# A hybrid encoder trunk on one core: first norm and turns re-ordered, tiles of x moved 384 columns apart

## The chip, the cores and the metric

The kernel runs on one core of a Trainium2 chip. The metric is the device time of one execution in microseconds, taken as the median of three runs. TensorE is called PE here, VectorE DVE, ScalarE ACT, GpSimd POOL and SyncE SP, as in the profile.

## The reference

Two layers, each a mixer and a squared-ReLU MLP, run over 1,024 prompt frames and 32 sample frames together, 1,056 columns in all. Cut to what matters:

```python
def trunk(x, ...):                      # DEPTH = 2, D_MODEL = 1024, D_FF = 4096
    for l in range(DEPTH):
        hn = rmsnorm(x, norm_mix_pre[l])
        m = mixer_even(hn, ...) if l % 2 == 0 else mixer_odd(hn, ...)
        x = x + rmsnorm(m, norm_mix_post[l])
        hn = rmsnorm(x, norm_ffn_pre[l])
        f = square(relu(hn @ mlp_up[l])) @ mlp_down[l]
        x = x + rmsnorm(f, norm_ffn_post[l])

def mixer_even(h, ...):                 # w_in: 1024 x 2048
    u, v, xb, gb = split(h @ w_in, 4)
    a_out = gelu(u) * spatial_gating(rmsnorm(gelu(v)))
    xc = causal_dwconv(xb, conv_w) + conv_b
    r, ig = sigmoid(xc @ wa + ba), sigmoid(xc @ wx + bx)      # block-diagonal
    log_a = -8 * r * softplus(-lam)
    h = scan(a=exp(log_a), b=sqrt(-expm1(2 * log_a)) * ig * xc)
    return concat(a_out, h * gelu(gb)) @ w_out

def mixer_odd(h, ...):                  # w_in: 1024 x 3072
    bg, cg, xv = split(h @ w_in, 3)
    return (bg * causal_dwconv(cg * xv)) @ w_out
```

## The kernel before

Activations lie transposed, features on the 128 partitions. The 1,056 columns are three tiles of 352 (`NT`, `TT`), the 1,024 features eight chunks (`KC`). Every float32 product is made of three passes in the faster `float32r` format: high weight by high x, high weight by low x, low weight by high x (L661 to L663). A **unit** is one output chunk of one tile: 8 x 3 = 24 matmuls of 128x352 into one of six PSUM banks. `plan()` lists 552 units and 184 weight panels. Most panels run over tiles 0, 1 and 2 in turn. Where a block starts or ends, four panels run together, first their tile 0, then tile 1, then tile 2 (a **tile block**). 104 of the 184 panels read the normed activations from `x_hi` and `x_lo` (16 of the even mixer, 32 of each MLP, 24 of the odd mixer). The rest read `h_hi` and `h_lo`. In each of the four buffers a chunk's row is `TS` = 1,088 columns, and tile t starts 352 t columns (1,408 t bytes) into it.

Each engine walks the units in order. The order of all else is written out by hand as tables of (unit, step), where step i follows the i-th of a unit's eight chunks: `COL_AT` (a norm's column sums on PE), `GATE_STEPS` (gate matmuls), `CONV_AT`, `DECAY_AT`, `SCAN_AT` (on DVE, with ACT's part), and the functions `even_unit`, `turn_before` and `turn_after`. An engine that waits in its program holds back all that stands behind it. For unit n DVE first evacuates the bank (`evacuate`), then makes the low part of a weight panel if one is due (`low`), then does what `even_unit` or `turn_after` names. PE needs the bank of unit n-6 evacuated and its panel's low part (`w_ready`).

A norm of x goes: ACT squares (`x_squares`), DVE sums eight chunks to one and folds them (`x_sum`, `rs_fold`), PE sums over the partitions (`col_sums`), ACT takes the root (`rs_root`), DVE the reciprocal and a transpose that spreads it (`rs_inverse`). x's own high and low parts are made beside this (`x_part` on ACT, `x_low` on DVE), since the norm's factor is applied when the bank is evacuated.

In the even mixer's beginning DVE convolves (`convolve`, 4 operations of 1,059 columns), PE makes six gate matmuls per group through one bank, each waiting until ACT has taken the sigmoid of the one before, ACT makes exp and tanh (`decays`), DVE the drive (`decay`), ACT a root (`drive_root`), DVE the scan. ACT's `gelu_panel(0)` works on units 12 to 14 and waits for their evacuation. `softplus` is 22 tiny dependent DVE operations. `BLOCK[b]` is the first unit of the last tile block before a turn to the next norm; s counts units from it, and s = 12 is the next phase's first unit.

Of the kernel before, what the change touches and what calls it, by code (L numbers as in the profile page):

```python
# [159 lines left out]
def build(nc, A, O):  # L161
# [27 lines left out]
    with ExitStack() as ctx:  # L189
# [51 lines left out]

        x_hi_raw = place("x_hi_raw", [P, KC * TS], F32, at_x_hi)
        x_old = place("x_old", [P, KC * TS], F32, at_x_lo)
# [5 lines left out]
        spare = [x_hi_raw[:, k * TS + TOK:k * TS + TOK + NJ] for k in range(KC)]  # L249
        fold, root, rcol = spare[0:6], spare[6], spare[7]  # L250
# [29 lines left out]
        v_out_s = place("v_out_s", [DEC, HALF], F32, at_h_lo + 8192)  # L280
# [151 lines left out]
        for b in range(4):  # L432
            for i, (what, t) in enumerate([("post", 0), ("post", 1), ("pre", 0), ("post", 2), ("pre", 1), ("pre", 2)]
# [17 lines left out]
        GATE_STEPS = (((10, 5), (11, 0), (11, 3), (11, 6), (12, 1), (12, 4)),  # L451
# [4 lines left out]
        DECAY_AT = (12, 17, 23, 31)  # L456
        SCAN_AT = (14, 18, 24, 32)
# [30 lines left out]

        block = ctx.enter_context(nc.Block())

        @block.sync
        def _(sp):
            def source(l):
                name, i = LOADS[l].name
                if name == "w_in_even":
                    return A[name][LOADS[l].col]
                w = A[name][i]
                return w[LOADS[l].row:LOADS[l].row + D, LOADS[l].col * P:LOADS[l].col * P + P]

# [19 lines left out]
            def first_half(l):  # L519
                sp.dma_start(W[l][2][:, 0:4, :], source(l)[:, 0:4, :]).then_inc(w_first[l], 16)  # L520
# [63 lines left out]
        def _(pool):  # L584
# [22 lines left out]
            for n in TMP_NO:  # L607
# [18 lines left out]
                else:  # L626
# [7 lines left out]
                                            ALU.subtract).then_inc(y_ready, 1)  # L634


        @block.tensor
        def _(pe):
# [133 lines left out]
            def warm_up(a):  # L772
                nc.tensor.matmul(ps[:, a, 0:TT], tmp[0][:, 0:P], tmp[0][:, :], start=True, stop=True)
# [62 lines left out]
        def _(act):  # L836
# [11 lines left out]
            def x_squares(u, t):  # L848
                for h in range(2):
                    if u > 0:  # L850
                        act.wait_ge(x_new, 6 * (u - 1) + 2 * t + h + 1)
                        dst = part(x_old, 4 * h, 4 * h + 4, t)
# [49 lines left out]
            def turn_before(n):  # L902

                for b in range(4):
# [16 lines left out]
                    if s == 13:  # L921
                        rs_root(b, "pre", 1)
                        x_squares(b + 1, 2)
                    if s == 15:
                        rs_root(b, "pre", 2)

            def turn_after(n):
                for b in range(3):
# [5 lines left out]
                    if s == 13:  # L934
                        x_part(b + 1, 2, 0, 8)
# [15 lines left out]
            x_squares(0, 1)  # L951
            act.wait_ge(consts, 3)
# [713 lines left out]
```

## Time and profile before

| | |
|---|---|
| median of 3 runs | 2172.08 us (2171.65 to 2172.17) |
| the profiled execution, its own time | 2171.2 us |
| its span | 2168.7 us |
| PE busy | 2153.3 us, 99% |
| DVE busy / ACT busy / POOL busy | 910.4 / 653.6 / 89.2 us |
| mean granted clock of PE | 0.998 |

The span runs from the first to the last instruction; 2.5 us of the execution lie around it. PE's busy share is an upper bound on its usefulness, since its matmuls overlap (each lasts some 320 ns and starts some 159 ns after the one before). The time that an extra wait costs is read from the starts.

### The profile page before, as it was taken

The numbers are of one execution on the slowest core, as the hardware profiler recorded it, in microseconds if no ns is written. First come the engines' busy times: TensorE is split into PE (matmuls) and PEld (weight loads), VectorE is DVE, ScalarE is ACT, GpSimd is POOL, SyncE is SP. The second block draws the span as 40 slices with busy tenths as digits, with TensorE's granted clock in tenths as the row PEclk, the third lists the DMA queues.
The fourth block names the chain that finished last, engine by engine and source line by source line (L and its number), as shares of the span: only waits on it lengthen the run. The fifth ranks groups of instructions, "written<-read, shape, count | busy, mean of one in ns | idle before, by whom it ended". The sixth has DMA issues, their size and how long they took to land.

```text
span 2168.7 us, 31484 instructions
## 1 busy us (share of the span) xinstructions
PE 2153.3 (99%) x13496; PEld 2140.8 (99%) x13496; DVE 910.4 (42%) x1438; ACT 653.6 (30%) x1105; POOL 89.2 (4%) x102
## 2 busy tenths in 40 slices
PE   8999999999999999999999999999999999999998
PEld 8999999999999999999999999999999999999998
DVE  7766367323322322333953333393223223322336
ACT  5673345202311320233511112353013103202332
POOL 0000000000000000000032332000000000000000
PEclk9999999999999999999999999999999999999999
DMA  4111422111111111132311113221111111111142
GB/s 159 34 37 40 139 76 83 50 49 44 45 49 49 44 45 49 49 104 74 114 49 46 49 49 130 66 92 53 46 50 49 41 48 49 49 40 49 49 139 81
DMA packets 208409, 138.64 MB, mean 64 GB/s; under 512 B 6000, under 2 KB 204784, under 8 KB 208272
## 3 DMA queue, kind: packets, MB, share of 16 engines
q1 hardware_dynamic: 207840, 136.04, 20.6%
q8 instruction: 107, 1.75, 0.3%
q10 hardware_dynamic: 432, 0.60, 0.1%
q14 instruction: 30, 0.25, 0.0%
HBM read 119.22 MB, written 17.40 MB: 63 GB/s over the span
## 4 chain that ended last, share of the span: by engine, by line
PE 96%; DVE 2%; issue 1%; ACT 1%; DMA 0%; DVEq 0%; SPq 0%; ACTq 0%
PE ps L661 31%; PE ps L662 31%; PE ps L663 31%; PE ps L736 1%; DVE x_lo L1228 1%; DVE x_old L1217 0%; PE ps L764 0%; DMA w_all_raw<-in_w_in_even_dram 0%; PE ps L692 0%; DVE f L1206 0%; PE ps L679 0%; PE ps L683 0%; PE ps L747 0%; DVE f L1199 0%; ACT L1032 0%
## 5 line engine op out<-in xcount | busy, mean ns | idle before, releaser
L661 PE MATMUL ps<-x_hi,w_all 128*128 128x352 f32 x2304 | 748.9, 325 | 0.0
L662 PE MATMUL ps<-x_lo,w_all 128*128 128x352 f32 x2304 | 740.7, 321 | 0.0
L663 PE MATMUL ps<-x_hi,w_all 128*128 128x352 f32 x2304 | 740.6, 321 | 0.0
L661 PE MATMUL ps<-h_hi,w_all 128*128 128x352 f32 x1728 | 556.2, 322 | 0.0
L663 PE MATMUL ps<-h_hi,w_all 128*128 128x352 f32 x1728 | 555.2, 321 | 0.0
L662 PE MATMUL ps<-h_lo,w_all 128*128 128x352 f32 x1728 | 555.2, 321 | 0.0
L661 PEld LDWEIGHTS ps<-x_hi,w_all 128*128 128x128 f32 x2304 | 432.9, 188 | 2.8 <-issue 0.3
L662 PEld LDWEIGHTS ps<-x_lo,w_all 128*128 128x128 f32 x2304 | 433.1, 188 | 2.4 <-issue 0.3
L663 PEld LDWEIGHTS ps<-x_hi,w_all 128*128 128x128 f32 x2304 | 432.9, 188 | 0.0
L839 ACT CAST w_all<-w_all_raw 128x1024 fp32r<-128x1024 f32 x166 | 173.4, 1044 | 531.9 <-DMA w_all_raw<-in_mlp_down_dram 324.2
L661 PEld LDWEIGHTS ps<-h_hi,w_all 128*128 128x128 f32 x1728 | 324.5, 188 | 0.3 <-DVE h_lo L1433 0.3
L662 PEld LDWEIGHTS ps<-h_lo,w_all 128*128 128x128 f32 x1728 | 324.5, 188 | 0.0
L663 PEld LDWEIGHTS ps<-h_hi,w_all 128*128 128x128 f32 x1728 | 324.4, 188 | 0.0
L1268 DVE SCALAR_TENSOR_TENSOR tmp<-ps,rstd 128x352 f32<-128x352 f32 x192 | 100.5, 524 | 424.6 <-PE ps L663 424.6
L898 ACT ACTIVATE tmp<-tmp 128x352 f32<-128x352 f32 x192 | 95.7, 498 | 473.0 <-DVE tmp L1268 472.5
L1274 DVE TENSOR_TENSOR f<-ps,f 128x352 f32<-128x352 f32 x144 | 75.4, 523 | 359.8 <-PE ps L663 359.8
L1167 DVE TENSOR_TENSOR w_all<-w_all_raw,w_all 128x1024 fp32r<-128x1024 f32 x166 | 202.1, 1217 | 14.7 <-ACT w_all L839 14.7
L1248 DVE TENSOR_TENSOR h_lo<-tmp,h_hi 128x352 fp32r<-128x352 f32 x192 | 99.0, 516 | 1.2 <-ACT h_hi L900 1.2
L900 ACT CAST h_hi<-tmp 128x352 fp32r<-128x352 f32 x192 | 93.6, 487 | 6.1
L1271 DVE COPY f<-ps 128x352 f32<-128x352 f32 x48 | 25.2, 525 | 138.0 <-PE ps L663 138.0
L1243 DVE TENSOR_TENSOR sq_sum<-sq_sum,tmp 128x352 f32<-128x352 f32 x83 | 43.3, 521 | 81.7 <-ACT tmp L891 79.7
L663 PE MATMUL ps<-h_hi,x_hi 128*128 128x352 f32 x192 | 61.7, 321 | 0.0
(192 smaller groups left out, 1430.9 us busy)
## 6 DMA issues: line engine op xcount, KB each, us to landing
w_all_raw<-in_mlp_up_dram SPq DMA_DIRECT2D x60, 512.0 KB, 3.9
w_all_raw<-in_mlp_down_dram SPq DMA_DIRECT2D x60, 512.0 KB, 3.7
x_save<-f SPq DMA_DIRECT2D x9, 1408.0 KB, 5.9
x_old<-x_save SPq DMA_DIRECT2D x9, 1408.0 KB, 11.6
w_all_raw<-in_c_w_in_dram SPq DMA_DIRECT2D x22, 512.0 KB, 3.6
w_all_raw<-in_w_in_even_dram SPq DMA_DIRECT2D x12, 512.0 KB, 3.5
x_old<-in_x_cols_dram SPq DMA_DIRECT2D x3, 1408.0 KB, 12.4
w_all_raw<-in_w_out_even_dram SPq DMA_DIRECT2D x6, 512.0 KB, 3.7
```

The source lines that it names most:

```text
L661: nc.tensor.matmul(dst, wh, hi, start=(i == 0), stop=False)
L662: nc.tensor.matmul(dst, wh, lo, start=False, stop=False)
L663: last = nc.tensor.matmul(dst, wl, hi, start=False, stop=(i == KC - 1))
L839: nc.scalar.copy(W[l][0], W[l][2]).then_inc(w_high, 1)
L898: nc.scalar.activation(tmp[n % 3][:, :], tmp[n % 3][:, :], ACT.Square).then_inc(h_sq, 1)
L900: nc.scalar.copy(pt(h_hi, u.m, u.t), tmp[n % 3][:, :]).then_inc(h_high, 1)
L1167: nc.vector.tensor_tensor(lo, raw, hi.bitcast(F32), ALU.subtract).then_inc(w_ready, 1)
L1243: nc.vector.tensor_tensor(dst, dst, tmp[n % 3][:, :], ALU.add).then_inc(f_acc, 1)
L1248: nc.vector.tensor_tensor(pt(h_lo, u.m, u.t), tmp[n % 3][:, :], pt(h_hi, u.m, u.t).bitcast(F32), ALU.subtract).then_inc(h_ready, 1)
L1268: ins = nc.vector.scalar_tensor_tensor(tmp[n % 3][:, :], bank(n), 0.0, scale, ALU.max, ALU.mult)
L1271: ins = nc.vector.tensor_copy(pt(f, m, t), bank(n))
L1274: ins = nc.vector.tensor_tensor(pt(f, m, t), bank(n), pt(f, m, t), ALU.add)
```

## The change

1. **First norm.** ACT makes x's high part of tile 2 before the first root. DVE evacuates the first four units, then does in one stretch the sum of tile 1, the low part of tile 2 and the sum of tile 2. `softplus` moves from unit 7 to unit 9. The first and third column sums move a step earlier and two steps later.
2. **Even mixer's beginning.** The first gates move from units 10 to 12 to units 11 to 13, the first `decays`/`decay` from 12 to 13, the first scan from 14 to 15. `gelu_panel(0)` stays at 14.
3. **Turns** (three of them). The squares of tile 2 go to the free h buffer and no longer onto `x_lo`'s place, so the low part need not wait for their sum; it goes first. ACT's root for tile 2 moves from s = 15 to 18, DVE's reciprocal from 15 to 20, PE's column sum from (20, 4) to (21, 5).
4. **Start.** The first two half panels are loaded by DMAs that ACT issues, around `vecs`; SP issues the rest.
5. **End.** Four small copies move from DVE to POOL.
6. **Layout.** In `x_hi` and `x_lo` a tile starts 384 columns (1,536 bytes) after the one before, a row is `XS` = 1,152 columns, and the sums of squares (`sq_sum`), `fold`, `root` and `rcol` live in the 32-column gaps. `h_hi`, `h_lo` and `f` keep their layout.

```diff
+XS = TOK + 96
-        x_hi = place("x_hi", [P, KC * TS], F32R)
+        x_hi = place("x_hi", [P, KC * XS], F32R)
-        x_lo = place("x_lo", [P, KC * TS], F32R)
+        x_lo = place("x_lo", [P, KC * XS], F32R)
-        spare = [x_hi_raw[:, k * TS + TOK:k * TS + TOK + NJ] for k in range(KC)]
-        fold, root, rcol = spare[0:6], spare[6], spare[7]
+        gap_hi, gap_lo = [b[:, :].rearrange("p (g n) -> p g n", g=NT * KC)[:, :, TT:TT + QUAD] for b in (x_hi_raw, x_old)]
+        sq_sum = (gap_hi[:, 0:NJ], gap_hi[:, NJ:2 * NJ], gap_lo[:, 0:NJ])
...
+        def tile_at(buf, t):
+            return t * (TT + QUAD if buf.shape[1] == KC * XS else TT)
...
-                     ("pre", 1): (16, 2), ("pre", 2): (20, 4)}
+                     ("pre", 1): (16, 2), ("pre", 2): (21, 5)}
-        COL_AT.update({(5, 1): (-1, "pre", 0), (7, 1): (-1, "pre", 1), (8, 5): (-1, "pre", 2)})
+        COL_AT.update({(5, 0): (-1, "pre", 0), (7, 1): (-1, "pre", 1), (8, 7): (-1, "pre", 2)})
-        GATE_STEPS = (((10, 5), (11, 0), (11, 3), (11, 6), (12, 1), (12, 4)),
+        GATE_STEPS = (((11, 4), (11, 7), (12, 2), (12, 5), (13, 0), (13, 3)),
-        DECAY_AT = (12, 17, 23, 31)
-        SCAN_AT = (14, 18, 24, 32)
+        DECAY_AT = (13, 17, 23, 31)
+        SCAN_AT = (15, 18, 24, 32)
...
             first_x(0, 0, 2, 0)
-            first_half(0)
             first_x(1, 2, 4, 0)
-            for l in range(1, 4):
-                first_half(l)
+            for l in range(2, 4):
+                first_half(sp, l)
...
+            first_half(act, 0)
             act.dma_start(vecs[:, :], A["vecs"]).then_inc(v_in, 16)
+            first_half(act, 1)
...
+                        if t == 2:
+                            act.wait_ge(pe_unit, START[u])
+                        dst = part((x_old, x_old, h_hi_raw)[t], 4 * h, 4 * h + 4, t)
...
             x_part(0, 1, 0, 8)
             x_squares(0, 1)
+            x_part(0, 2, 0, 8)
             act.wait_ge(consts, 3)
             rs_root(-1, "pre", 0)
-            x_part(0, 2, 0, 8)
             x_squares(0, 2)
...
-                if n == 0:
+                if n == 3:
                     x_sum(0, 1)
-                if n == 1:
                     x_low(0, 2, 0, 8)
-                if n == 2:
+                    x_sum(0, 2)
                     rs_inverse(-1, "pre", 1)
-                if n == 3:
-                    x_sum(0, 2)
                 if n == 7:
+                    rs_inverse(-1, "pre", 2)
+                if n == 9:
                     softplus()
-                    rs_inverse(-1, "pre", 2)
...
-                    if s == 15:
+                    if s == 20:
                         rs_inverse(b, "pre", 2)
...
                     if s == 14:
-                        x_sum(b + 1, 2)
                         x_low(b + 1, 2, 0, 8)
                         if UNITS[n - 1].kind == "up":
                             h_low(n - 1)
+                    if s == 15:
+                        x_sum(b + 1, 2)
```

**DVE, the first units, before.** Evacuations of the first twelve units write `xb_pad`; `sq00` and `sq01` are the squares of tiles 2 and 1 (tile 0's too, earlier), `x_lo` the low parts, the RECIPROCAL the third norm's, `soft` the first row of `softplus`, `lru0` the first convolution, `w_all` the low part of panel 4, which unit 12 needs.

```order
L1280 TENSOR_TENSOR xb_pad_79<-ps,rstd_57 128x352
L1217 TENSOR_TENSOR sq01_75<-sq01_75 128x1408
...
L1228 SCALAR_TENSOR_TENSOR x_lo_50<-f_53,vecs_64,x_hi_49 128x352 x8
...
L1217 TENSOR_TENSOR sq00_74<-sq00_74 128x1408
...
L1186 TENSOR_REDUCE x_hi_raw_70<-sq_sum_56 128x11
L1280 TENSOR_TENSOR xb_pad_79<-ps,rstd_57 128x352 x4
L1148 TENSOR_SCALAR soft_65<-soft_65 128x4
...
L1173 RECIPROCAL x_hi_raw_70<-x_hi_raw_70 128x11
L1175 STREAM_TRANSPOSE rstd_57<-x_hi_raw_70 128x352
L1280 TENSOR_TENSOR xb_pad_79<-ps,rstd_57 128x320
...
L1349 TENSOR_SCALAR lru0_86<-xb_pad_79,vecs_64 128x1059
...
L1167 TENSOR_TENSOR w_all_54<-w_all_raw_55,w_all_54 128x1024
```

**The same engine and place, in the change.** Line numbers are those of the changed kernel.

```order
L1291 TENSOR_TENSOR xb_pad_78<-ps,rstd_59 128x352 x4
L1230 TENSOR_TENSOR sq01_74<-sq01_74 128x1408
...
L1241 SCALAR_TENSOR_TENSOR x_lo_50<-f_53,vecs_63,x_hi_49 128x352 x8
L1230 TENSOR_TENSOR sq00_73<-sq00_73 128x1408
...
L1200 TENSOR_REDUCE x_old_70<-x_old_70 128x11
L1187 RECIPROCAL x_old_70<-x_old_70 128x11
...
L1291 TENSOR_TENSOR xb_pad_78<-ps,rstd_59 128x352 x4
L1187 RECIPROCAL x_old_70<-x_old_70 128x11
...
L1360 TENSOR_SCALAR lru0_85<-xb_pad_78,vecs_63 128x1059
...
L1162 TENSOR_SCALAR soft_64<-soft_64 128x4
...
L1181 TENSOR_TENSOR w_all_54<-w_all_raw_55,w_all_54 128x1024
```

Four evacuations stand together ahead of both sums, and `softplus` and with it everything behind stands between the first convolution and panel 4's low part.

**ACT, units 12 to 16, before.** `lru3`, `lru1` are exp and tanh (L988, L990) and then the root (L995) of the first group; `tail` the copies of conv rows; `gelu0` is `gelu_panel(0)`; the CAST is a weight panel's high part; `ig1` the first gate of the second group (L979).

```order
L988 ACT_TABLE_LOAD
L988 ACTIVATE lru3_89<-lru1_87,soft_65 128x1059
L990 ACTIVATE lru1_87<-lru1_87,soft_65 128x1059
L839 CAST w_all_54<-w_all_raw_55 128x1024
L995 ACT_TABLE_LOAD
L995 ACTIVATE lru1_87<-lru1_87 128x1059
L967 COPY tail_66<-xb_pad_79 128x3
...
L1032 ACT_TABLE_LOAD
L1032 ACTIVATE gelu0_93<-gelu0_93 128x1056
L839 CAST w_all_54<-w_all_raw_55 128x1024
L979 ACT_TABLE_LOAD
L979 ACTIVATE ig1_92<-ps,vecs_64 128x353 x2
```

**The same in the change.** The root of the first group (L1009) now stands behind the gelu (L1046), which waits for unit 14's evacuation; DVE has the first `decay` ahead of that evacuation, where before it had it ahead of unit 13's.

```order
L1002 ACT_TABLE_LOAD
L1002 ACTIVATE lru3_88<-lru1_86,soft_64 128x1059
L1004 ACTIVATE lru1_86<-lru1_86,soft_64 128x1059
L981 COPY tail_65<-xb_pad_78 128x3
...
L1046 ACT_TABLE_LOAD
L1046 ACTIVATE gelu0_92<-gelu0_92 128x1056
L1009 ACT_TABLE_LOAD
L1009 ACTIVATE lru1_86<-lru1_86 128x1059
L849 CAST w_all_54<-w_all_raw_55 128x1024
L993 ACT_TABLE_LOAD
L993 ACTIVATE ig1_91<-ps,vecs_63 128x353 x2
```

**DVE, a turn, before:** from the evacuation of unit s = 14 (`tmp2`) on. `x_old` holds the squares of tile 2, `x_lo` gets tile 2's low parts, the RECIPROCAL is `rs_inverse(b, "pre", 2)`, and the row behind it is unit s = 15's evacuation.

```order
L1268 SCALAR_TENSOR_TENSOR tmp2_60<-ps,rstd_57 128x352
L1217 TENSOR_TENSOR x_old_71<-x_old_71 128x4x352
...
L1219 TENSOR_TENSOR sq_sum_56<-x_old_71 128x352
L1186 TENSOR_REDUCE x_hi_raw_70<-sq_sum_56 128x11
L1228 SCALAR_TENSOR_TENSOR x_lo_50<-f_53,vecs_64,x_hi_49 128x352 x8
L1248 TENSOR_TENSOR h_lo_52<-tmp1_59,h_hi_51 128x352
L1173 RECIPROCAL x_hi_raw_70<-x_hi_raw_70 128x11
...
L1268 SCALAR_TENSOR_TENSOR tmp0_58<-ps,rstd_57 128x352
```

**The same in the change.** The low parts stand ahead of the sum, the squares are in `h_hi_raw`, and the RECIPROCAL has moved behind the evacuation of unit s = 19.

```order
L1279 SCALAR_TENSOR_TENSOR tmp2_58<-ps,rstd_59 128x352
L1241 SCALAR_TENSOR_TENSOR x_lo_50<-f_53,vecs_63,x_hi_49 128x352 x8
L1259 TENSOR_TENSOR h_lo_52<-tmp1_57,h_hi_51 128x352
L1279 SCALAR_TENSOR_TENSOR tmp0_56<-ps,rstd_59 128x352
...
L1230 TENSOR_TENSOR h_hi_raw_71<-h_hi_raw_71 128x4x352
...
L1233 TENSOR_TENSOR x_old_70<-h_hi_raw_71 128x11x32
L1200 TENSOR_REDUCE x_old_70<-x_old_70 128x11
L1279 SCALAR_TENSOR_TENSOR tmp1_57<-ps,rstd_59 128x352
...
L1187 RECIPROCAL x_old_70<-x_old_70 128x11
```

## Rows read from the trace of the kernel before

**Rows 1.** The page, busy time, share of the span and instructions of PE.

```profile
PE 2153.3 (99%) x13496; PEld 2140.8 (99%) x13496; DVE 910.4 (42%) x1438; ACT 653.6 (30%) x1105; POOL 89.2 (4%) x102
```

**Rows 2.** Timeline, PE, 39 to 62 us: start, us, what, idle before and releaser.

```profile
42.99 0.36 PE L723 MATMUL ps<-x_hi_raw,quads 128*128 128x11 f32 x2 [1.16 <-issue]
...
55.61 1.51 PE L736 MATMUL ps<-lru,gate_w 128*128 128x353 f32 x2 [4.54 <-issue]
```

**Rows 3.** Windows: length, busy of PE, PEld, DVE, ACT, POOL, granted clock, DMA.

```profile
53.40:60.20 6.80, 4.59 (x13) 3.87 (x14) 3.85 (x7) 1.49 (x2) 0.00 (x0) 0.50 0.09 7
```

**Rows 4.** Windows over two units of tile 0, then three of tile 1.

```profile
328.81:336.41 7.60, 7.60 (x51) 7.60 (x49) 7.31 (x13) 5.73 (x11) 0.00 (x0) 1.00 0.77 235
340.45:351.97 11.52, 11.52 (x74) 11.52 (x73) 10.83 (x14) 7.88 (x13) 0.00 (x0) 1.00 0.34 127
```

**Rows 5.** Timeline, ACT, around the first root.

```profile
28.05 0.27 ACT L845 ACTIVATE x_hi_raw<-ps,eps 128x11 f32<-128x11 f32 x1 [4.11 <-PE ps L723]
28.22 3.94 ACT L866 ACTIVATE x_hi<-f,vecs 128x352 fp32r<-128x352 f32 x8
```

**Rows 6.** Timeline, DVE, 28 to 60 us.

```profile
28.61 0.55 DVE L1175 STREAM_TRANSPOSE rstd<-x_hi_raw 128x352 f32<-128x352 f32 x1
...
33.70 4.04 DVE L1228 SCALAR_TENSOR_TENSOR x_lo<-f,vecs,x_hi 128x352 fp32r<-128x352 f32 x8
...
39.22 2.53 DVE L1217 TENSOR_TENSOR sq<-sq 128x1408 f32<-128x1408 f32 x2
...
42.82 1.78 DVE L1280 TENSOR_TENSOR xb_pad<-ps,rstd 128x352 f32<-128x352 f32 x4
...
48.98 0.23 DVE L1173 RECIPROCAL x_hi_raw<-x_hi_raw 128x11 f32<-128x11 f32 x1
...
50.60 0.83 DVE L1349 TENSOR_SCALAR lru<-xb_pad,vecs 128x1059 f32<-128x1059 f32 x1
...
55.42 0.58 DVE L1280 TENSOR_TENSOR xb_pad<-ps,rstd 128x320 f32<-128x320 f32 x2
...
59.42 1.22 DVE L1167 TENSOR_TENSOR w_all<-w_all_raw,w_all 128x1024 fp32r<-128x1024 f32 x1
```

**Rows 7.** Timeline, PE, two gate matmuls of unit 16.

```profile
82.50 0.75 PE L736 MATMUL ps<-xc,gate_w 128*128 128x353 f32 x2
...
84.53 0.76 PE L736 MATMUL ps<-xc,gate_w 128*128 128x353 f32 x2
```

**Rows 8.** Timeline, DVE, the first drive.

```profile
70.71 1.25 DVE L1358 TENSOR_TENSOR lru<-lru,lru 128x1059 f32<-128x1059 f32 x1
...
73.22 1.26 DVE L1363 SCALAR_TENSOR_TENSOR lru<-lru,lru 128x1059 f32<-128x1059 f32 x1 [0.58 <-ACT lru L990]
...
77.61 0.52 DVE L1292 TENSOR_TENSOR gelu<-ps,rstd 128x352 f32<-128x352 f32 x1
```

**Rows 9.** Timeline, ACT, gelu, a panel's cast, a table load, the first gate of unit 16.

```profile
79.73 1.09 ACT L1032 ACTIVATE gelu<-gelu 128x1056 f32<-128x1056 f32 x1 [0.74 <-DVE gelu L1292]
81.41 1.05 ACT L839 CAST w_all<-w_all_raw 128x1024 fp32r<-128x1024 f32 x1 [0.59 <-DMA w_all_raw<-in_w_in_even_dram]
82.48 1.28 ACT L979 ACT_TABLE_LOAD   x1
83.78 0.56 ACT L979 ACTIVATE ig<-ps,vecs 128x353 f32<-128x353 f32 x1
```

**Rows 10.** Timeline, PE, first turn, from unit s = 20 to s = 21.

```profile
355.88 0.32 PE L663 MATMUL ps<-x_hi,h_lo 128*128 128x352 f32 x1
356.36 0.40 PE L661 MATMUL ps<-x_hi,h_hi 128*128 128x352 f32 x1 [0.16 <-DVE tmp L1268]
```

**Rows 11.** Timeline, DVE, the four small copies of the end.

```profile
2162.08 0.73 DVE L1599 COPY row_rstd<-x_hi_raw 32x2 f32<-32x2 f32 x4
```

**Rows 12.** Timeline, POOL, two products of the same shape in the odd mixer.

```profile
1156.49 0.96 POOL L630 TENSOR_TENSOR cy<-tmp,cy 128x352 f32<-128x352 f32 x1 [6.68 <-DVE cy L1483]
...
1159.02 1.97 POOL L630 TENSOR_TENSOR cy<-tmp,cy 128x352 f32<-128x352 f32 x1
```

More of the change, by code:

```diff
@@ L240, in build @@
         last_rstd = row_rstd[:, 0:2]
-        x_hi_raw = place("x_hi_raw", [P, KC * TS], F32, at_x_hi)
-        x_old = place("x_old", [P, KC * TS], F32, at_x_lo)
+        x_hi_raw = place("x_hi_raw", [P, KC * XS], F32, at_x_hi)
+        x_old = place("x_old", [P, KC * XS], F32, at_x_lo)
         h_hi_raw = place("h_hi_raw", [P, KC * TS], F32, at_h_hi)
         h_lo_raw = place("h_lo_raw", [P, KC * TS], F32, at_h_lo)
-        spare = [x_hi_raw[:, k * TS + TOK:k * TS + TOK + NJ] for k in range(KC)]
-        fold, root, rcol = spare[0:6], spare[6], spare[7]
+        gap_hi, gap_lo = [b[:, :].rearrange("p (g n) -> p g n", g=NT * KC)[:, :, TT:TT + QUAD] for b in (x_hi_raw, x_old)]
+        sq_sum = (gap_hi[:, 0:NJ], gap_hi[:, NJ:2 * NJ], gap_lo[:, 0:NJ])
+        fold = [gap_lo[:, NJ + i, 0:NJ] for i in range(6)]
+        root, rcol = gap_lo[:, NJ + 6, 0:NJ], gap_lo[:, NJ + 7, 0:NJ]
         sq0 = [place(f"sq0{i}", [P, KC, TT], F32, at_h_lo + i * KC * TT * 4) for i in range(2)]
@@ L279, in build @@
                 cy.append(place(f"cy{n}{i}", [P, TOK], F32, at + 2 * TOK * 4 + 2 * c_step + i * TOK * 4))
-        v_out_s = place("v_out_s", [DEC, HALF], F32, at_h_lo + 8192)
+        v_out_s = place("v_out_s", [DEC, HALF], F32, at_h_lo + 13056 + HALF * 4)
         def chunk_buf(bufs, c):
@@ L487, in send_rows, with source, first_half @@
                 eng.dma_start(O["y_rows"][i, :, h * HALF:(h + 1) * HALF], result_rows(i, h)).then_inc(out_dma, 16)
+        def source(l):
+            name, i = LOADS[l].name
+            if name == "w_in_even":
+                return A[name][LOADS[l].col]
+            w = A[name][i]
+            return w[LOADS[l].row:LOADS[l].row + D, LOADS[l].col * P:LOADS[l].col * P + P]
+        def first_half(eng, l):
+            eng.dma_start(W[l][2][:, 0:4, :], source(l)[:, 0:4, :]).then_inc(w_first[l], 16)
         block = ctx.enter_context(nc.Block())
@@ L634, in _ @@
                                             ALU.subtract).then_inc(y_ready, 1)
+            pool.wait_ge(inverted, NORM[3, "post", 2] + 1)
+            for b in range(4):
+                nc.gpsimd.tensor_copy(last_rstd[b * QUAD:(b + 1) * QUAD, :],
+                                      rcol[b * QUAD:(b + 1) * QUAD, 3 + b::4]).then_inc(last_r, 1)
         @block.tensor
@@ L772, in warm_up @@
             def warm_up(a):
-                nc.tensor.matmul(ps[:, a, 0:TT], tmp[0][:, 0:P], tmp[0][:, :], start=True, stop=True)
+                nc.tensor.matmul(ps[:, a, 0:TT], rstd[:, 0:P], rstd[:, 0:TT], start=True, stop=True)
             def out_rows(i, a):
@@ L1212, in squares @@
                 def squares(k0, k1):
-                    return part(x_old, k0, k1, t) if u > 0 else sq0[t % 2][:, k0:k1, :]
+                    return part((x_old, x_old, h_hi_raw)[t], k0, k1, t) if u > 0 else sq0[t % 2][:, k0:k1, :]
                 for i, h in enumerate((4, 2)):
@@ L1218, in x_sum @@
                     dve.wait_ge(x_tree, n + i + 1)
-                nc.vector.tensor_tensor(sq_sum[:, t * TT:(t + 1) * TT].unsqueeze(1), squares(0, 1), squares(1, 2), ALU.add
-                                        ).then_inc(x_acc, 1)
+                a, c = [squares(k, k + 1).rearrange("p o (j c) -> p (o j) c", c=QUAD) for k in range(2)]
+                nc.vector.tensor_tensor(sq_sum[t], a, c, ALU.add).then_inc(x_acc, 1)
                 rs_fold(u - 1, "pre", t)
             def x_low(u, t, k0, k1):
-                if u > 0:
+                if u > 0 and t < 2:
                     dve.wait_ge(x_acc, 3 * u + t + 1)
@@ L1319, in second_low @@
                                         ).then_inc(w_ready, 1)
-            nc.vector.memset(tmp[0][:, :], 0.0).then_inc(warm, 1)
+            nc.vector.memset(rstd[:, 0:TT], 0.0).then_inc(warm, 1)
             dve.wait_ge(w_first[0], 16)
@@ L1597, in _ @@
             nc.vector.tensor_tensor(c, c, part(x_old, 0, KC, 2, 0, LAST_COLS), ALU.add).then_inc(x_new, 1)
-            for b in range(4):
-                nc.vector.tensor_copy(last_rstd[b * QUAD:(b + 1) * QUAD, :],
-                                      rcol[b * QUAD:(b + 1) * QUAD, 3 + b::4]).then_inc(last_r, 1)
             dve.wait_ge(last_r, 4)
```

53 lines of the change are left out of this document (19 added, 34 removed).

## The prediction

> **What bounds the kernel now.** I read the busy times first: PE is busy 99% of the span [rows 1], and no other engine comes to half of it. So every part of the change has to be told by the starts of PE's matmuls. Where these stand at their steady distance nothing done on DVE, ACT or POOL counts. The second view was the windows by tile. Two units of tile 0 take 7.60 us, 3.80 a unit or 158.4 ns a matmul. Three units of tile 1 take 11.52 us, 3.84 a unit or 160.0 ns [rows 4]. The busy share is full in both, so this is a pace and no wait, and the difference, 0.040 us a unit, goes with the tile whose row starts 1,408 bytes into the chunk. The third view was the timeline of the first 90 us, where PE does wait: 1.16 us ahead of the column sum at (8, 5) and 4.54 us ahead of the gate at (10, 5) [rows 2]. Around and behind the second the granted clock is 0.50 for 6.80 us in which PE worked 4.59 us [rows 3], so half of that work, 2.3 us, is lost as well. Last come the turns, where one start is late by 0.48 - 0.16 = 0.32 us behind an evacuation [rows 10], and the end, where four small copies take 0.73 us on DVE [rows 11].
>
> **Beginning, first half.** I followed DVE's new order with the durations of before. The first root started at 28.05, behind a column sum [rows 5]. ACT now makes the eight high parts of tile 2 (3.94 us) ahead of it, in the 4.11 us that it stood idle, so they cost nothing and the squares of tile 2 are ready earlier. With the column sum one step earlier the reciprocal and transpose (28.61 to 29.16 before) end at about 28.9. Then on DVE: four evacuations 1.8 to 30.7; a sum with its fold 3.6 (2.53 for its two large additions, the rest for the last addition and the fold) to 34.3; eight low parts 4.0 to 38.3; the second sum 3.6 to 41.9 [rows 6]. The column sum now stands at (8, 7). PE would have reached (8, 5) at 42.99 - 1.16 = 41.8; two chunks of 0.48 later, and 0.2 earlier for the start, is 42.6. So the 1.16 us wait goes, and PE enters unit 9 at 42.8. DVE goes on: reciprocal, transpose and four evacuations 2.6 to 44.5; then reciprocal, transpose and the evacuation of unit 8, another 1.6 with PE's column sum waited for at 42.6, to 46.1; the first convolution 4.8 (50.60 to 55.42) to 50.9. The gate at (11, 4) is reached at 42.8 + 7.6 + 2.4 = 52.8, behind that: the 4.54 us wait goes too [rows 2, 6].
>
> **A wait takes its place.** Unit 12 needs the low part of panel 4, and `softplus` now stands ahead of it. Between 44.6 and 48.98 DVE did `softplus` and nothing else, 4.4 us [rows 6]. So: evacuation of unit 9 to 51.4, `softplus` to 55.9, evacuation of 10 to 56.4, low part 1.22 to 57.6. A gate adds (84.53 - 82.50) - 9 x 0.16 = 0.6 us to PE [rows 7]. PE comes to unit 12 at 42.8 + 7.6 + 3.8 + 1.2 = 55.4 and waits until 57.75, **2.4 us**.
>
> **A second wait.** Units 12 and 13 take 10.0 with two gates each: PE is through unit 13 at 67.75. DVE: its evacuation to 68.4, the low part of panel 6 to 69.5, the first `decay` 6.3 us (70.71 to about 77.0, its 0.58 us wait for ACT included) to 75.85, the evacuation of unit 14 to 76.35 [rows 8]. Before, this `decay` stood ahead of unit 13's evacuation, with the same gelu behind unit 14's. ACT: the gelu 1.09 to 77.45; a table load of 1.28 and the root, of 1,059 columns too, 1.09 to 79.85; the cast 1.05 to 80.9; another table load 1.28 to 82.2; the second group's first gate 0.56 to 82.75 [rows 9]. PE's next gate, (16, 4), needs that one's bank: it starts at 82.85. PE is there at 67.75 + 7.6 + 3.0 = 78.35, and waits **4.5 us**. Queued behind ACT's gelu are the root, the cast and every gate's sigmoid, and behind PE's gate the whole of unit 16. The same gate stood at 84.53 before [rows 7]. So of the 6.2 us (84.53 - 78.35) that the first half gives, **1.7 are left**.
>
> **The clock.** Before, PE lost 2.3 us to the half clock, and all of it lies ahead of the gate of unit 16, so it is in the 84.53 already. The new 4.5 us wait can bring a fall of its own behind it: nothing (the 1.16 us wait brought none) to 2.3 us (as much as the 4.54 us wait did, of like length) [rows 2, 3]. The fall of before began some 2.3 us into the idle time and reached 4.6 us past it, so I take **+1.5**. The 2.4 us wait ahead of unit 12 lies between 1.16 and 4.54. A fall there is absorbed by the second wait, up to 4.5 us, so it costs 0.
>
> **Pace.** In the change tile 1 starts 1,536 bytes into a chunk's row. 104 panels read `x_hi` and `x_lo`, and each has one unit of tile 1. Five of them (four in the first block, and unit 13) lie ahead of the second wait, which swallows what they gain. If the tile's place in memory sets the pace, 99 x 0.040 = **-4.0 us** [rows 4]. The bounds are 0 (the pace belongs to the tile's number or its output) and -4.0. I take the whole, since everything else about the two kinds of unit is the same: the weights, the number of columns, the engine loads. The products of `h_hi` and `h_lo` keep their places and their pace.
> The Trainium skill has a rule that speaks against this term: "TensorE: Matmul & The Clock Gate", section "Back-to-back issue gap", puts the distance of two warm matmuls at their columns over 2.4 plus 2.5 ns, with nothing about where the moving rows lie. That would be an estimated 149 ns for both tiles and no gain; the rows show 158.4 and 160.0, so the rule does not describe the difference that is there.
>
> **Turns.** The row shows a start 0.32 us late, since the evacuation of s = 15 stands behind the RECIPROCAL, and that behind ACT's root [rows 10]. In the change the low parts do not wait for the sum, and the RECIPROCAL has gone to s = 20. Three turns like this give 1.0, and the shorter stretch of DVE before it some more at the start of the same block (0 to 0.2 each): **-1.2** (bounds 0, if the sum at s = 15 makes another evacuation late, and -1.6). The column sum now stands at (21, 5), five units or 19 us after the evacuation of s = 15; the sum and its fold, 3.6 us, and ACT's root lie between the two, and that distance hides them.
>
> **End.** The four copies, 0.73 us [rows 11], leave DVE. POOL has nothing else to do there, and may make them while DVE still multiplies, or 0.73 us in parallel and then be waited for. **-0.7** at best; the low bound is 0. POOL's product took 1.97 us beside DVE's two-input operation and 0.96 alone [rows 12], so POOL may be the later one.
> The Trainium skill, "SBUF — State Buffer", section "SBUF: two separate sides", says that GpSimd and a two-input operation of DVE lock each other out of the shared port. The trace agrees (0.96 against 1.97). By that rule the copies would overlap DVE's last large additions badly and the term would be some -0.2 by estimate.
>
> **Start.** Two half panels of 256 KB go out from ACT rather than from SP. The bytes are the same and PE's first matmul waits for the last of them: 0 to -0.5, I take -0.2, which runs through the whole chain above.
>
> **Sum.** Against the execution's own 2171.2 us, of which the median of 2172.1 is 0.9 more: -1.7 - 0.2 + 1.5 - 4.0 - 1.2 - 0.7 = -6.3, so 2164.9 of its own and **2165.8 us** as a median. A measurement of this kernel tells about 0.2%, 4.3 us: the edges are 2167.7 and 2176.4.
>
> **Rivals.**
> - The second wait does not come (`decay` or the gelu is through earlier than I count, or the chain behind the gelu is shorter). Then the beginning gives 6.2 us and no clock is lost: 2172.1 - 6.4 - 4.0 - 1.2 - 0.7 = 2159.8. For it: my chain has eleven links. Against it: each has its row. 0.13.
> - The layout changes no pace: 2165.8 + 4.0 = 2169.8. For it: the rows show only that pace goes with tile. 0.12.
> - The clock falls as deep and long at both waits as before, and the second fall is not covered: 2.3 rather than 1.5 behind it, and 1.7 more where the first fall outlasts the slack: 2168.3. 0.09.
> - Slower: 1,408 is not what costs, but any start other than one that follows the last row without a gap, or the longer row itself. All tiles of x then take 3.84 us: 208 units of tiles 0 and 2 x 0.040 = +8.3 in place of -4.0, so 2178.1. It decides from a pace of tiles 0 and 2 above 3.83 us, where the loss outweighs the other terms and the edge of 0.2% (4.3 us, and 2.3 for the gain of the other terms, are 6.6 over 208 units, 0.032 each). Against it: tile 2 starts 2,816 bytes in and has tile 0's pace. 0.04.
>
> **How the numbers follow.** The forecast has 0.62; its own range is 2163.5 to 2168.0 (start and end terms at zero; clock 0 to 2.3). The whole range, 2159.8 to 2169.9, takes in the case without a second wait and the case of no change in pace. Faster: 0.62 less a little, 0.13, and a third of the clock's case, 0.78; within 0.2%: 0.17; slower 0.05.
>
> **What would show it.** PE's starts at units 12 and (16, 4): idle 2.4 and 4.5 us, the first behind DVE's low part, the second behind ACT's gate, with no idle time at (8, 7) and (11, 4). The window over three units of tile 1 of an x panel: 11.40 us rather than 11.52. The start after s = 20: 0.16. PE's clock behind the second wait. In the end DVE's last additions followed by less than 0.73 us. I am wrong if the first `softplus` row is not followed by a wait of unit 12, if ACT's gelu of unit 14 isn't late, or if tile 1 keeps 3.84.

## The result, and the profile after

The changed kernel takes 2191.78 us (median of 4 runs, 2191.51 to 2192.01), against 2171.86 us beside it. The ratio is 1.0093, with a 95% interval of 1.008 to 1.0106: **slower by 0.9%**, some 20 us, where 2165.8 was forecast with a range up to 2169.9.

The page, busy time, share of the span and instructions, as in [rows 1]:

```profile
PE 2176.1 (99%) x13496; PEld 2164.0 (99%) x13496; DVE 911.5 (42%) x1434; ACT 652.5 (30%) x1105; POOL 90.8 (4%) x106
```

PE has the same number of instructions and is busy all the time, 22.8 us longer. So the loss is no wait. Windows over whole units of the changed kernel, with the columns of [rows 3]:

```profile
371.57:403.57 32.00, 32.00 (x194) 32.00 (x193) 11.06 (x19) 11.68 (x20) 0.00 (x0) 1.00 0.17 50
1164.97:1196.97 32.00, 32.00 (x193) 32.00 (x193) 8.19 (x15) 4.79 (x9) 10.46 (x10) 1.00 0.17 50
...
511.32:522.72 11.40, 11.40 (x75) 11.40 (x73) 3.14 (x5) 2.92 (x5) 0.00 (x0) 1.00 0.17 47
```

The first two windows are eight units each of x, in the first MLP and in the odd mixer. They take 4.00 us a unit, tiles 0, 1 and 2 alike, at a granted clock of 1.00. The third is one panel of x in the first MLP's second group, with the same instructions on the same buffers: 3.80 us a unit, and tile 1's among them, where [rows 4] had 3.84. Away from the column sums the starts of the slow units stand 165 to 168 ns apart, 166.7 on average. Timeline, PE, changed kernel, in the odd mixer:

```profile
1164.97 0.33 PE L671 MATMUL ps<-x_hi,w_all 128*128 128x352 f32 x1
1165.14 0.33 PE L672 MATMUL ps<-x_lo,w_all 128*128 128x352 f32 x1
1165.31 0.33 PE L673 MATMUL ps<-x_hi,w_all 128*128 128x352 f32 x1
1165.47 0.33 PE L671 MATMUL ps<-x_hi,w_all 128*128 128x352 f32 x1
```

So PE has three rhythms here: 158.4 ns (its distances go 155, 159, 158, 162), an even 160.0, and an even 166.7. The third was in the trace of before too, for part of one unit of tile 2 (the ninth), and I had not looked at it. Timeline, PE, kernel before:

```profile
39.51 0.33 PE L663 MATMUL ps<-x_hi,w_all 128*128 128x352 f32 x1
39.68 0.33 PE L661 MATMUL ps<-x_hi,w_all 128*128 128x352 f32 x1
39.84 0.33 PE L662 MATMUL ps<-x_lo,w_all 128*128 128x352 f32 x1
40.01 0.33 PE L663 MATMUL ps<-x_hi,w_all 128*128 128x352 f32 x1
```

In the change the slow stretches are units 71 to 96 (into the first MLP), 263 to 336 (the whole odd mixer) and 359 to 384. Each begins behind the column sum at s = 10 of a turn and ends at the first unit of h's tile 1. Between the two spans, 2168.7 and 2190.1 us, the difference is made up like this (from the start of each unit's first matmul in the two traces):

| part | us |
|---|---|
| start: first steady unit later | +0.44 |
| from there to the end of the even mixer's input (unit 47) | +1.45 |
| 120 units of x at 4.00, with the turns that lie in them | +20.6 |
| 6 units of h at 4.00 | +1.2 |
| 48 free units of x's tile 1, 3.80 for 3.84 | -1.9 |
| behind the last unit | -0.3 |
| sum | +21.4 |

The two waits of the beginning came where they were forecast, the first at half its size. Timelines of the changed kernel, PE at unit 12 and at the gate (16, 4), ACT's gelu, root, cast and first gate behind it:

```profile
58.06 0.43 PE L671 MATMUL ps<-x_hi,w_all 128*128 128x352 f32 x1 [1.15 <-DVE w_all L1181]
...
83.13 1.54 PE L746 MATMUL ps<-xc,gate_w 128*128 128x353 f32 x2 [4.22 <-ACT ig L993]
```

```profile
76.79 1.08 ACT L1046 ACTIVATE gelu<-gelu 128x1056 f32<-128x1056 f32 x1 [4.01 <-DVE gelu L1303]
77.89 1.28 ACT L1009 ACT_TABLE_LOAD   x1
79.19 1.08 ACT L1009 ACTIVATE lru<-lru 128x1059 f32<-128x1059 f32 x1
80.18 1.03 ACT L849 CAST w_all<-w_all_raw 128x1024 fp32r<-128x1024 f32 x1
81.22 1.28 ACT L993 ACT_TABLE_LOAD   x1
82.52 0.56 ACT L993 ACTIVATE ig<-ps,vecs 128x353 f32<-128x353 f32 x1
```

The gate stands at 83.13 (forecast 82.85), 1.4 us ahead of [rows 7]. Behind it the clock falls; windows, changed kernel:

```profile
78.50:88.62 10.12, 5.90 (x21) 4.79 (x19) 8.10 (x7) 5.68 (x7) 0.00 (x0) 0.69 0.00 0
```

From that gate to the start of unit 17 PE took 5.5 us at a granted clock of 0.50, where before it took 2.8 at 1.00. That is 2.7 us for the clock, of which I had put down 1.5. So unit 17 starts 1.28 us later than before, instead of earlier.

### The profile page after: what moved, and what is told of

The parts are those of the page before. It is cut to its first block, busy times and chain, and to the rows that moved or that the text cites. A ratio compares the mean times of both kernels' runs of the same rounds, so it can differ in the third digit from the quotient of the medians.

```text
span 2190.1 us, 31486 instructions
## 1 busy us (share of the span) xinstructions
PE 2176.1 (99%) x13496; PEld 2164.0 (99%) x13496; DVE 911.5 (42%) x1434; ACT 652.5 (30%) x1105; POOL 90.8 (4%) x106
## 4 chain that ended last, share of the span: by engine, by line
PE 97%; DVE 2%; ACT 1%; issue 0%; DVEq 0%; ACTq 0%
PE ps L671 32%; PE ps L672 31%; PE ps L673 31%; PE ps L746 1%; PE ps L774 0%; PE ps L783 0%; PE ps L689 0%; PE ps L693 0%; PE ps L702 0%; DVE sq L1230 0%; DVE xb_pad L1291 0%; PE ps L757 0%; DVE x_lo L1241 0%; DVE lru L1364 0%; PE ps L733 0%
## 5 line engine op out<-in xcount | busy, mean ns | idle before, releaser
L672 PE MATMUL ps<-h_lo,x_hi 128*128 128x352 f32 x192 | 61.9, 322 | 0.0
```

The lines of the kernel that those rows point to most:

```text
L672: nc.tensor.matmul(dst, wh, lo, start=False, stop=False)
```

## The experiments

All addresses below are counted from the kernel's first buffer, and what is said of them is their remainder by 256 bytes. In before, x's and h's tiles stand at 0, 128, 0, and all weights at 128, but for the first block's fourth panel, at 0. In the change x's three tiles stand at 0; h and the weights are as before. `quads`, the weights of a column sum, stands at 32 before and at 128 in the change.

**Order alone, layout alone.** Two kernels: `order_only` is the change without its layout, `layout_only` before with nothing but that layout.

> The change's whole order (beginning, turns, start, end) on the layout of before: tiles of x 352 columns apart, sums of squares in a buffer of their own. Theory A (the layout does the harm: with every tile of x a whole number of 256 bytes from its chunk's start, PE's rhythm falls after a column sum into one of 166.7 ns a matmul and no tile-1 unit frees it): no unit of the first MLP or the odd mixer at 4.00 us, tile 1 at 3.84 again, about +1.3 us from the beginning, -1.1 from the turns, 2172.5 us in all. Theory B (the re-ordered turns let it in): the same 120 units at 4.00 us, about 2193 us.

> The new layout alone (tiles 384 columns apart, rows of 1,152, sums in the gaps), with before's order everywhere. Theory A: units 71 to 96, 263 to 336 and 359 to 384 at 4.00 us as in the change, +21.8 for them, -2.0 for the free tile-1 units, about 2192 us. Theory B: no unit at 4.00 us, every tile 3.80, about 2168 us.

`order_only`: 2171.1 us, ratio 0.9996 (0.9986 to 1.0005), every x unit at 3.80 or 3.84. So the re-ordering as a whole is worth nothing beyond the noise. In its trace two parts cancel: unit 17 starts 0.4 us later than before, and from unit 48 on the turns give 1.6 us. Unit 12 is waited for 1.82 us there. `layout_only`: median 2186.24, ratio 1.0053 (1.0032 to 1.0074), with executions from 2174 to 2195 us (one of 6411 us, and one of before of 4341 us, are left out of the ratios). The loss is the layout's, though not a fixed one: this kernel spreads over 21 us where the others of these comparisons agree within 5.

**The layout alone, a second profile.**

> The new layout alone on before's order once more, for a profile of an execution of ordinary length (its nine times ran from 2174 to 2195 us with one far outside). Theory A (with all tiles of x alike, a rhythm entered at a restart is never left before the next h tile 1): each stretch of x's units from a turn to the end of its phase stands as a whole at 4.00 or at 3.80 us a unit, and which it is differs from execution to execution; the time follows from the stretches: 2169 + 14 for the odd mixer + 4.6 for each MLP.

This execution took 2172.08 us. Its slow stretches are short: units 71 to 80, 263 to 272, 359 to 368. Timeline, PE, `layout_only_2`, inside unit s = 20 and the first matmuls of s = 21:

```profile
356.99 0.33 PE L664 MATMUL ps<-x_hi,h_hi 128*128 128x352 f32 x1
357.16 0.33 PE L665 MATMUL ps<-x_lo,h_hi 128*128 128x352 f32 x1
357.33 0.32 PE L666 MATMUL ps<-x_hi,h_lo 128*128 128x352 f32 x1
357.78 0.40 PE L664 MATMUL ps<-x_hi,h_hi 128*128 128x352 f32 x1
358.02 0.32 PE L665 MATMUL ps<-x_lo,h_hi 128*128 128x352 f32 x1
358.18 0.32 PE L666 MATMUL ps<-x_hi,h_lo 128*128 128x352 f32 x1
```

PE goes at 0.167 until 357.33, then starts 0.45 later, and from there at 158 ns. This is the late evacuation of [rows 10], the wait that the re-ordered turns take away. My expectation was that a stretch is slow or fast as a whole; it is not. A small pause can end it, and does so in all three turns of this execution. Not every interruption does: in the change the column sums at s = 13, 16 and 21 stand inside the slow stretch (the matmuls around them start 304 and 248 ns apart instead of 167), and 166.7 goes on behind each.

**Layout with the new turns.** Everything else is before's.

> The new layout and the re-ordered turns, with before's beginning, start and end. Theory A2 (the layout lets the slow rhythm stand; PE's wait of some 0.3 us at s = 21, which the new turns take away, was what ended it in the executions of the layout alone): units 71 to 96, 263 to 336 and 359 to 384 at 4.00 us in every execution, 2172 + 21.8 - 2.0 - 1.1 = 2191 us, with a spread of under 1 us. Rival (the turns have no part in it): as the layout alone, executions anywhere from 2172 to 2195 us.

2191.64 us (2190.93 to 2191.85), ratio 1.0094 (1.0077 to 1.0111): units 71 to 96, 263 to 336 and 359 to 384 slow, in executions within 1 us of each other. Windows, `layout_turns`, three units of the odd mixer:

```profile
1164.84:1176.84 12.00, 12.00 (x74) 12.00 (x73) 3.39 (x5) 3.46 (x6) 6.09 (x6) 1.00 0.16 45
```

So the turns, good for 0.3 us or more each by themselves, take away the pause that had at times ended the slow rhythm. The two parts of the change together cost more than the layout alone.

**Does the place set the pace?** Two kernels move x's buffers by 128 bytes (everything behind them by 256), in the change and in before.

```diff
+        at_byte[0] += 128
         at_x_hi = at_byte[0]
 ...
+        at_byte[0] += 128
         at_h_hi = at_byte[0]
```

> The changed kernel with x_hi and x_lo moved 128 bytes up and everything behind them 256 bytes, so that all three tiles of x start at an odd multiple of 128 bytes, as tile 1 alone did before, and h's tiles keep theirs. If the place within 256 bytes sets the pace of x's units: 3.84 us (160.0 ns a matmul) for all three tiles, none at 4.00, so -16 for the 120 slow units and +5.8 for the 144 that ran at 3.80: about 2181 us. If row length, gap or order set it: 4.00 us in the same 120 units and about 2192 us.

> The kernel before with x_hi and x_lo moved 128 bytes up and everything behind them 256 bytes; nothing else. If the place within 256 bytes sets the pace: x's units of tiles 0 and 2 take 3.84 us and those of tile 1 3.80, h's stay as they are: 208 x 0.04 - 104 x 0.04 = +4.2, about 2176 us. If the tile's number or its output sets it: no change, 2172 us.

`after_off`: 2181.41 us, x's units all at 3.84 in the MLPs and the odd mixer. `before_off`: 2178.09 us, ratio 1.0032 (1.0019 to 1.0045). Windows, `before_off`, the same panel of the odd mixer over its tiles 0, 1 and 2:

```profile
1196.93:1200.77 3.84, 3.84 (x26) 3.84 (x25) 1.30 (x2) 0.49 (x1) 3.18 (x3) 1.00 0.48 137
1200.77:1204.57 3.80, 3.80 (x26) 3.80 (x25) 0.53 (x1) 1.53 (x3) 1.29 (x2) 1.00 0.00 0
1204.57:1208.41 3.84, 3.84 (x26) 3.84 (x25) 1.66 (x2) 0.00 (x0) 0.00 (x0) 1.00 0.01 4
```

The tiles have changed roles: [rows 4] had 3.80 for tile 0 and 3.84 for tile 1. The place does set the pace. The 2 us above expectation are mostly 16 units of h at 4.00 (60 to 62, 67 and their like in the four turns). Some panels of h have their weights in x's buffer, and these had moved with it: unit 67 reads such a panel, and units 60 to 62 stand behind one.

**Against what?** The change, with the rotating weights and what lies behind them moved instead of the rows:

```diff
-        at_byte[0] += 128
         at_w = at_byte[0]
```

> The changed kernel without the 128 bytes between f and w_all, so that the weights of the rotating slots start at whole multiples of 256 bytes as x's tiles do, and nothing of the activations moves. If it is the place of moving rows against that of the weights that sets the pace: x's units on rotating slots 3.84 us and none at 4.00, h's tiles 0 and 2 on them 3.84 and h's tile 1 3.80, so -18 for the slow units, +8 for the free x units, +3 for h: about 2184 us. If only the moving rows' own place counts: as the changed kernel, 2192 us with 120 units at 4.00.

2183.32 us, ratio 1.0051 (1.0035 to 1.0068). Windows, `weights_off`, three x units of one panel, and h's tiles 0 and 1:

```profile
1200.57:1212.09 11.52, 11.52 (x74) 11.52 (x74) 3.45 (x5) 2.02 (x4) 4.45 (x4) 1.00 0.16 46
1548.08:1551.92 3.84, 3.84 (x26) 3.84 (x25) 0.52 (x1) 0.00 (x0) 0.00 (x0) 1.00 0.49 137
1551.92:1555.72 3.80, 3.80 (x27) 3.80 (x25) 0.53 (x1) 1.05 (x1) 0.00 (x0) 1.00 0.02 4
```

No row of x or h moved, and yet x is at 160 on all rotating slots and h's tiles have changed roles. So it is the place of the moving rows *against that of the weights*. Where both stand at the same place within 256 bytes, PE goes at 160.0. Where they stand 128 apart, it goes at 158.4 or at 166.7, and stays in either. This holds for all thirteen profiles of ordinary length. From unit 48 on, all 2,271 units with both at the same place are at 160.0. Of the 4,281 units with 128 between them 3,755 are at 158.4, 514 at 166.7, and 12 come out near 160, nine of them with a column sum in them. Other distances than 0 and 128 were not tried.

**What ends and what begins the slow rhythm?** In the change the third rotating slot alone goes 128 bytes up, so that x's panels on it are of the 160 kind:

```diff
-        w_all = place("w_all", [P, 6, D], F32R)
+        w_all = place("w_all", [P, 4, D], F32R)
+        at_byte[0] += 128
+        w_p2 = place("w_p2", [P, 2, D], F32R)
```

> The changed kernel with the third rotating slot alone moved 128 bytes up, so that every third panel of x has weights that stand to x's rows as they did to tile 1's before. If such a unit frees the slow rhythm: the x panels on that slot take 3.84 us, those on the other two 3.80, and no stretch of 4.00 is longer than two panels: about 2173 us. If the slow rhythm is a matter of the layout as a whole: units on the other two slots stay at 4.00 in the same stretches and the time is above 2185 us.

2202.91 us, ratio 1.014 (1.0125 to 1.0155): the slowest of all. Windows, `p2_off`, an MLP's panel on the second slot (after units of h), then one on the moved slot, then two on the others:

```profile
880.04:891.45 11.41, 11.41 (x75) 11.41 (x74) 3.14 (x5) 2.92 (x5) 0.00 (x0) 1.00 0.16 46
891.45:902.97 11.52, 11.52 (x74) 11.52 (x74) 4.01 (x7) 3.91 (x7) 0.00 (x0) 1.00 0.16 47
902.97:926.95 23.98, 23.98 (x145) 23.98 (x145) 8.02 (x14) 7.82 (x14) 0.00 (x0) 1.00 0.16 44
```

3.80, then 3.84, then six units at 4.00. A unit of the 160 kind does end a slow stretch, and no stretch is longer than two panels; that much was right. But such a unit also starts the next one, when the weights' place changes behind it while the rows' place stays. In before the 160 kind comes with tile 1, where the rows' place changes, and its next unit falls to 158.4. The thirteen profiles bear both out. Where a unit of the 160 kind is followed by one of the other kind because the *rows'* place changed, that one is at 158.4 in 1,281 of 1,285 cases. Where the *weights'* place changed, it is at 166.7 in 83 of 95 cases (`p2_off`, `weights_off`, `before_off`, `after_off`). The short slow stretches of the change's beginning (units 4 to 6 and 8 to 10) stand behind such a change of weights too, the panel at place 0. My time for this kernel was 30 us off, since I had no term for a new entry.

**What lets it in at s = 10?** The last matmuls of unit s = 10 behind the column sum stand 299, 247, 161 ns apart in the slow kernels and 303, 246, 162 in before. The same column sum; but `quads` stands elsewhere. (The column sum at s = 8, in units of the same kind, leaves 158.4 in all of them, with `quads` at 128 too. So the place alone is not enough, and what sets s = 10 apart from s = 8 was not tried.) So the change with `quads` where it was, within 256 bytes:

```diff
+        at_byte[0] += 160
         ident = place("ident", [P, P], F32)
         quads = place("quads", [P, P], F32)
```

> The changed kernel with ident, quads and what lies behind them 160 bytes up, so that the column sums' weights stand at the same place within 256 bytes as before. In the kernel before the same column sum at s = 10 goes back to 158 ns, in the change to 166.7. If the place of quads decides which rhythm follows a column sum: no unit at 4.00 us, 2192 - 21.8 = 2170 us. If not: units at 4.00 as in the change, 2192 us.

2167.34 us (2165.27 to 2168.97), ratio 0.998 (0.9971 to 0.999): **24.4 us less than the change**, by 160 bytes that nothing uses. It is also 3.8 us less than `order_only`, which differs from it by the layout alone: with the slow rhythm kept out, the layout gives what was forecast for it (-4.0). Windows, `quads_off`, three units in the odd mixer:

```profile
1190.80:1202.20 11.40, 11.40 (x74) 11.40 (x73) 3.53 (x5) 2.02 (x4) 4.51 (x4) 1.00 0.17 47
```

And before, with `quads` where the change has it (96 bytes more ahead of it):

> The kernel before with quads and what lies behind it 96 bytes up, so that the column sums' weights stand at the place within 256 bytes that they have in the change; nothing else. If that place lets the slow rhythm in after the column sum at s = 10: units 71 to 75 (three turns) at 4.00 us, and the first unit of tile 1 ends it, since here tile 1 stands at an odd multiple of 128 bytes: 5 x 0.2 = +1.0 us a turn, no long stretch, about 2175 us. If quads' place matters only together with the new layout: 2172 us.

2174.76 us, ratio 1.0013 (1.0003 to 1.0022). Windows, `before_quads`, the four units of x's tile 0 in the first turn, and one of tile 1 behind them:

```profile
320.90:337.10 16.20, 16.20 (x99) 16.20 (x99) 15.10 (x23) 8.44 (x15) 0.00 (x0) 1.00 0.40 122
341.17:345.01 3.84, 3.84 (x26) 3.84 (x25) 3.84 (x4) 0.42 (x1) 0.00 (x0) 1.00 0.00 0
```

Four units at 4.00 (and 0.2 for the column sum in one of them), then tile 1 at 3.84, which has ended it. Units 71 to 75, 263 to 267 and 359 to 363 are slow as expected; two turns have a second short stretch (273 to 276, 369 to 372), which I had not foreseen. It begins behind the column sum at s = 20. In all three turns the matmuls go over to 167 ns there, and the late evacuation follows with a start 0.45 us after the one before. In the first turn 158 follows it, in the other two 167 goes on. So such a pause can end the slow rhythm and need not.

**A beginning that keeps its gain.** `mix` has before's layout, gates, first `decay`, first scan and start, with the change's sums, low parts, `softplus`, turns and end.

> The layout of before, start's loads as before, and of the change the new order of sums and low parts, softplus at unit 9, the turns and the end; the gates, decay(0) and scan(0) stay at before's units (10 to 12, 12, 14). By the chain: the first gate waits about 2.2 us for the convolution instead of 4.5, unit 12 is entered at about 57.6, decay(0) starts some 5 us sooner, and the gate (16, 4) stands at about 77 to 78 rather than 84.5: about -6.5, with -1.1 from the turns and -0.3 from the end some 2164.5 us. If the waits of the beginning only move on: 2171 us.

2162.96 us (2162.59 to 2163.52), ratio 0.9957 (0.9942 to 0.9972). Timeline, PE, `mix`, the only wait of over 0.4 us between 38 and 90 us, and the gate (16, 4):

```profile
51.32 0.83 PE L743 MATMUL ps<-lru,gate_w 128*128 128x353 f32 x2 [1.26 <-issue]
...
78.12 0.86 PE L743 MATMUL ps<-xc,gate_w 128*128 128x353 f32 x2
```

The gate stands 6.4 us ahead of [rows 7], with no clock lost.

**The best of both.** `mix_layout` is `mix` with the change's layout and `quads` 160 bytes up.

> The layout of the change with the order of the kernel called mix (new sums, low parts, softplus, turns and end; gates, decay(0), scan(0) and the start's loads as before), and quads 160 bytes up. If quads' place keeps the slow rhythm out: 2163 - 4.0 = 2159 us with every unit of x at 3.80. If it does not: 2163 - 2 + 21.8 = 2183 us.

2158.7 us (2158.26 to 2159.58), ratio 0.9943 (0.9928 to 0.9958), the fastest here, and 33 us below the change. Against `mix` the layout gives 4.3 us here.

## Why the prediction was wrong

**Pace: the step that failed.** The prediction said "the bounds are 0 ... and -4.0" and took the whole, "since everything else about the two kinds of unit is the same". The measured term is +20.6 + 1.2 - 1.9, some +20, and with the turns' gain taken out of the slow units nearer +22. The gain of 0.04 us on each of tile 1's units is real (`quads_off`, `mix_layout`), but the term had no price for the other rhythm that the same places allow, and nothing above 0 as an upper bound. Two things were wrong in it.
- 3.84 was taken as a penalty on tile 1's place. It is one of two relations between rows and weights, and the other has two rhythms of its own, 158.4 and 166.7. [Rows 4] shows only the better one. `weights_off` and `before_off` show the relation.
- Tile 1's units had a second part: at before's places each of them ends a slow stretch, if there is one. The layout that made them faster by 0.04 took that away, and a stretch that would have lasted five units lasted 74. `before_quads` shows the one (+2.9 us), the change the other (+20).
That `quads` went to another place was in the kernels' difference (`sq_sum` and 32 bytes of padding ahead of it are gone), and I gave it no price. `quads_off` and `before_quads` show that this shift of it and what lies behind it is what lets the slow rhythm in at s = 10. Whether it is `quads` itself or a smaller buffer behind it was not tried apart; the column sum reads only `quads` of them.
The Trainium skill, "TensorE: Matmul & The Clock Gate", section "Back-to-back issue gap", gives the formula that the prediction used as the gap of an isolated matmul, an estimated 149 ns here, and says that in a stream of weight loads and matmuls both set the distance. The rows have 158.4, 160.0 and 166.7 for the same instruction at clock 1.00, all above the estimate; neither statement tells them apart or accounts for the 20 us.

**The rivals.** "Slower" had the right sign with a wrong mechanism: it priced all of x at 3.84 (+8.3), which is what `after_off` and `weights_off` do. 2178.1 was its time, and these two took 2181.4 and 2183.3. The case of no change in pace came closest to `order_only`, 2171.1 for 2169.8. The case without a second wait is what `mix_layout` builds on purpose: 2158.7 for 2159.8.

**Beginning: right in mechanism, off in two sizes.** Each link of DVE's and ACT's chain came within 0.6 us. The wait at unit 12 was 1.15 rather than 2.4 us: PE came later by the start's 0.4 and by six of units 4 to 10 at 4.00. The second was 4.22 for 4.5. The clock cost 2.7 and not 1.5; the estimate from when the fall of before began was too mild, and 2.3, my upper end, would have been the better choice. Unit 17 starts 1.28 us late, where the terms made it 0.4 early. (The upper edge of the forecast's own range does not follow from what it names: start and end at zero and the clock at 2.3 make 2167.5 and not 2168.0.)

**Start: probably the wrong sign.** PE's first matmul on data is at 6.80 and was at 6.20; that alone says little, since it is at 6.80 in `mix` too, with before's start. Timeline, PE, changed kernel:

```profile
6.80 1.63 PE L689 MATMUL ps<-x_hi,w_all 128*128 128x352 f32 x4
```

Its first steady unit (unit 4) starts at 23.3 to 23.6 us in all six kernels with the change's start, and at 22.6 to 23.2 in the seven others profiled at ordinary length. So the two DMAs from ACT seem to cost about 0.5, where I took -0.2 and had 0 as the upper bound. No run moves them alone.

**Turns: right.** The 0.48 us start behind s = 20 is gone. The 120 slow units alone would make +22.4 (80 x 0.20 and 40 x 0.16); they make 20.6, so the turns gave 1.8 where I took 1.2. `order_only`, with no unit slow, has 1.6 directly.

**End: right in its step, half lost behind it.** Timelines, changed kernel, DVE's and then POOL's:

```profile
2182.92 0.99 DVE L1607 TENSOR_TENSOR f<-f,x_old 128x768 f32<-128x768 f32 x1
2183.83 2.71 DVE L1615 SCALAR_TENSOR_TENSOR x_old<-ps,row_rstd,x_old 128x512 f32<-128x512 f32 x4
```

```profile
2181.57 1.52 POOL L643 COPY row_rstd<-x_old 32x2 f32<-32x2 f32 x4 [827.17 <-DVE x_old L1597]
```

From the last reciprocal to L1615 DVE now takes 2.55 us, and took 3.28: the 0.73 of [rows 11]. POOL's four copies take 1.52 us beside DVE, twice as long, and are still in time. But the span ends only 0.3 us sooner against PE's last unit, as it does in `order_only`, `quads_off`, `mix` and `mix_layout`. The other 0.4 is lost behind DVE's last additions: from their end to the end of the span it is 3.6 us (3.4 in those four), and was 3.1. What takes it there was not looked into.

## What to carry to other kernels

A layout change moves every buffer that comes after it, and in this stream of back-to-back matmuls the relative place of moving rows and weights set the pace. List the addresses, modulo 256 bytes, of all that PE reads, the small constants too, before and after. Look in the trace for every distance between matmul starts that occurs, the rare ones above all: what is rare may be so because something else ends it. And what looks like a small cost (tile 1's 0.04 us, a 0.3 us pause) may be what keeps a larger one short, so try such parts apart.

## What was not expected of the hardware

- For the same 128x352 float32r matmul at clock 1.00 the distance is 160.0 ns where rows and weights have the same place within 256 bytes, and 158.4 or 166.7 where they are 128 bytes apart. Both of these can last for a whole phase: 74 units, 1,776 matmuls, at 166.7.
- A switch from "same place" to "128 apart" gives 158.4 when the rows' place changed (1,281 of 1,285 cases) and mostly 166.7 when the weights' did (83 of 95).
- Which of the two follows the column sum (two 11-column matmuls) at s = 10 goes with 96 or 160 bytes of padding ahead of its weights: 158.4 at place 32, 166.7 at 128, in all three turns of the nine profiles in which x, h and the weights of the panels were not moved against each other in some other way. The column sum at s = 8 leaves 158.4 in either case.
- A start late by 0.3 us can turn 166.7 into 158.4 and need not (in the first turn of `before_quads` it does, in the other two not); a column sum inside the slow rhythm did not in the change. Where that wait was there, executions of one kernel spread from 2172 to 2195 us; without it they agreed within 1 us, all slow.
